# One step list reordered: the second sample pass's states, keys and values move from unit 5's u rows to its v rows, and its output norms go ahead of the attention

## The chip, the cores and the metric

The kernel runs on one core of one Trainium2 chip. The metric is device time in microseconds (us) of one execution. The kernel before was timed three times: 4341.75, 4350.58 and 4363.11 us, median 4350.58.

## The reference, cut to what matters

Two groups of tokens, a prompt of 128 and a sample of 512, run through two layers with shared weights. For the kernel these are four passes: p = 0 prompt layer 0, p = 1 sample layer 0, p = 2 prompt layer 1, p = 3 sample layer 1. A layer computes

```
h   = rmsnorm(x) * (1 + scale1) + shift1 ; proj = h @ w_in
o_f, o_b = chunk_gla(q, logf, v, S0)           # gated recurrence, forward and backward, 8 heads of 64x64 state
o   = rmsnorm(o_f + o_b) * silu(gate)          # the "output norm"
ckv = rmsnorm(ckv_raw); k_nope, v_att = ckv @ w_kvb    # keys and values from the latents
attn = softmax(q_nope k_nope + q_pe k_pe) v_att
x   = x + gate1 * (concat(o, attn) @ w_out)
h2  = rmsnorm(x) * (1 + scale2) + shift2
x   = x + gate2 * peer(h2)                     # 8 heads x 16 experts per token: rows of u and of v
```

The expert layer takes, for each token, 128 rows of the table u (a dot product each) and 128 rows of v (a weighted sum). All is float32.

## The kernel before, in words

Tokens are worked in tiles of 128, called units. Pass 0 is unit 0, pass 1 units 1 to 4, pass 2 unit 5, pass 3 units 6 to 9. Unit 5 is thus the prompt tile of layer 1; beside its expert rows the sample's layer 1 (pass 3) is prepared, as pass 1 is beside the rows of unit 0.

The expert rows are the backbone of the time. For each unit 128 gathers of u rows and then 128 of v rows are issued by GpSimd, each an indirect DMA of 128 rows of 4 KB into one of ten slots (`ring`, L853). VectorE reads a landed u slot in one multiply-reduce (`dots`, L1818) and so frees it; TensorE reads landed v slots in chunks of two (`sum_v`, L1170, eight recorded matmuls a chunk) and so frees them. This gives two stages for a unit: the u stage, paced by VectorE or the gathers, and the v stage, paced by TensorE or the gathers.

All other work, called trunk here, is woven between these rows by hand. `plan()` builds one list of steps (`PLAN`). Every engine walks that same list in order and does its part of each step, so the list fixes the order within each engine, while semaphores order the engines against each other. `beside_u[u]` and `beside_v[u]` name the trunk steps of the stages of unit u, each with a weight. `spread(a, b)` puts both lists on a line from 0 to 1 by their weights, each step at its middle, and merges them: 64 row steps of two rows each beside a trunk of total weight W lie W/64 apart. `spread_pairs(a, b)` merges two trunk lists and gives every step the weight 3.

The steps that the change touches:

- `keys_values(p)`: `wb` and `stores` (SyncE only; `wb` loads the attention's weights and waits for the last scan alone), `hgS` (VectorE carries the states over the tiles, L1628 and L1629), four `hgo` (TensorE applies the states, L1017, VectorE adds the result to `o`, L1641), `latT` (TensorE turns the normed latents, L901, ScalarE copies), `kn` (keys, L1041) and `va` (values, L1050), both TensorE with ScalarE copies. Weights 5 + 4 x 2 + 12 + 12 + 9 = 46.
- `outputs(p)`: four `hgfin`, the output norm of a tile: seven VectorE operations (L1653 to L1660) and a root on ScalarE. Weight 4 each.
- `keys_values_outputs(p)`: the same steps, two norms between `kn` and `va` and two after. It is used already for pass 1, beside the rows of unit 0.
- `attention(p, t)`: `q` (queries), then for eight heads `sc` (scores), `pt` (turned probabilities) and `pv` (sum over values). Weight 48.
- `("keys", p)`: SyncE loads the expert sub-keys over the attention's weights (L817), after a wait for the last `va` step; the next tiles of w_out stand behind it in SyncE's queue.
- `decided(p)`: `joined` (gate row L913, output projection, norm), eight steps of the expert query projection, two score steps, and eight top-k steps on VectorE, four of them between the two scores. Weight 138.

Of the kernel before, what the change touches and what calls it, by code (L numbers as in the profile page):

```python
# [32 lines left out]
N_IN, N_OUT, N_WQ = 26, 8, 16  # L33
# [36 lines left out]
def modulations(l, lo, hi):  # L70

    out = []
    for j in range(lo, hi):
        out.append((("ada", l, j), 1.5))
        if j % (3 * SECT) == 2 * SECT - 1:
            out.append((("adafin", l, j // (3 * SECT)), 1))
    return out


def norms(p, b):  # L80

    out = []
    for t in range(*BATCHES[p][b]):
        out += [(("rms", p, t, 0), 4), (("norm", p, t, 0), 4)]
    return out


def projections(p, b, lo=0, hi=N_IN):

    t0, t1 = BATCHES[p][b]  # L90
    out = [(("inp", p, b, j), 2 * max(1, (t1 - t0) * 0.9)) for j in range(lo, hi)]
    if hi == N_IN:
        out.append((("fgate", p, b), 4))
        out += [(("small", p), 0)] if b == 0 else []
        out += [(("rows", p), 0), (("latn", p), 3 + 3 * NT[p])] if b == len(BATCHES[p]) - 1 else []
    return out
# [12 lines left out]
def scans(p, t0, t1):  # L109

    return [(("hg", p, t, m), 4) for t in range(t0, t1) for m in range(LV)]


def keys_values(p):

    nt, g = NT[p], PASSES[p][0]
    out = [(("wb", p), 0), (("stores", p), 0)] if p else []
    if g:
        out += [(("hgS", p), 5)] + [(("hgo", p, t), 2) for t in range(nt)]
    return out + [(("latT", p), 3 * nt), (("kn", p), 12 if g else 4), (("va", p), 9 if g else 2)]  # L120


def keys_values_outputs(p):

    steps, gated = keys_values(p), outputs(p)
    half = (len(gated) + 1) // 2
    return steps[:-1] + gated[:half] + steps[-1:] + gated[half:]


def outputs(p):  # L130

    return [(("hgfin", p, t), 4) for t in range(NT[p])]


def attention(p, t):

    out = [(("q", p, t), 8), (("sc", p, t, 0), 2), (("sc", p, t, 1), 2), (("pt", p, t, 0), 2)]
    for hh in range(H):
        if hh + 2 < H:
            out.append((("sc", p, t, hh + 2), 2))  # L140
        out.append((("pv", p, t, hh), 1))
        if hh + 1 < H:
            out.append((("pt", p, t, hh + 1), 2))
    return out
# [7 lines left out]
def joined(p, t):  # L152

    tiles = served(p, t)
    return [(("outp", p, t, i), 5 * len(tiles)) for i in range(N_OUT // WCH)] \
        + [step for a in tiles for step in ((("rms", p, a, 1), 4), (("norm", p, a, 1), 6))]


def searched(p, t):

    return [(("wq", p, t, i), 5 * len(served(p, t))) for i in range(N_WQ // WCH)] \
        + [(("score", p, t, i), 3) for i in range(2)]


def queries(p, t):

    return joined(p, t) + searched(p, t)


def choice(p, t):  # L170

    u = U0[p] + t
    return [(("topk", u, hh), 7.5) for hh in range(H)] + [(("soft", u), 2)]


def opened(p):

    steps, heads = searched(p, 0), choice(p, 0)
    half = N_WQ // WCH // 2
    first, second, scores = steps[:half], steps[half:2 * half], steps[2 * half:]  # L180
    return joined(p, 0) + first + scores[:1] + heads[:1] + second[:2] + heads[1:2] + second[2:] + scores[1:]


def decided(p):

    steps, heads = searched(p, 0), choice(p, 0)
    half = N_WQ // WCH // 2
    first, second, scores = steps[:half], steps[half:2 * half], steps[2 * half:]
    return joined(p, 0) + first + scores[:1] + woven(heads[:4], second) + scores[1:] + heads[4:]


def spread(a, b, until=1.0):

    def placed(steps):
        total, at, out = sum(us for _, us in steps), 0.0, []
        for step, us in steps:
            out.append(((at + us / 2) / total, step))
            at += us
        return out

    merged = sorted([(x, 0, i, step) for i, (x, step) in enumerate(placed(a))]
                  + [(x * until, 1, i, step) for i, (x, step) in enumerate(placed(b))])
    return [step for _, _, _, step in merged]


def spread_pairs(a, b):

    return [(step, 3) for step in spread(a, b)]


def woven(a, b):

    us = dict(a + b)
    return [(step, us[step]) for step in spread(a, b)]


def first_unit():

    heads, rows = choice(0, 0), [(("u", 0, c), 2.6) for c in range(NCU)]
    ahead, beside = 2 * (H - 2), NCU * 17 // 20  # L220
    opening = []
    for hh in range(2, H):
        opening += rows[2 * (hh - 2):2 * (hh - 1)] + heads[hh:hh + 1]
    levels = scans(1, 0, NT[1])
    ends, last = LV - 1, (NT[1] - 1) * LV
    trunk = woven(levels[:ends], late_projections(1, LATE, 16)) \
        + woven(levels[ends:last + 3], late_projections(1, 16, N_IN)) + late_latents(1) + levels[last + 3:]
    return [("hp", 0)] + spread(opening + heads[H:], projections(1, 0, 0, LATE)) + [("fgate", 1, 0)] \
        + spread(rows[ahead:beside], trunk) + spread(rows[beside:], keys_values_outputs(1))


def plan():

    def alone(steps):
        return [step for step, _ in steps]

    first = modulations(0, 0, 2 * SECT)
    rms, norm = norms(0, 0)
    inputs = projections(0, 0)
    out = alone(first[:4] + [(("x0",), 0)] + first[4:12] + [rms] + first[12:] + [norm] + inputs[:6]  # L240
                + [(("rest",), 0)] + inputs[6:12] + [(("wb", 0), 0)])
    out += spread(inputs[12:N_IN], norms(1, 0)) + alone(inputs[N_IN:])
    out += spread(scans(0, 0, 1), modulations(0, 2 * SECT, 3 * SECT))
    out += spread(keys_values(0) + [(("keys", 0), 0)] + spread_pairs(attention(0, 0), outputs(0)),
                  modulations(0, 3 * SECT, N_ADA))
    out += alone([(("stores", 0), 0)] + opened(0))
    prompt_q = queries(2, 0)
    beside_u = {1: attention(1, 1) + queries(1, 1)[:-2],
                2: spread_pairs(attention(1, 3), modulations(1, N_ADA // 2, N_ADA)) + queries(1, 2),
                3: keys_values(2) + spread_pairs(attention(2, 0), outputs(2)) + [(("keys", 1), 0), (("score", 1, 3, 0), 3), (("score", 1, 3, 1), 3)],  # L250
                4: norms(3, 0) + projections(3, 0),
                5: norms(3, 1) + projections(3, 1, 0, 12) + [(("fgate", 3, 1), 4)]
                + woven(scans(3, 3, 4), projections(3, 1, 12, N_IN)[:N_IN - 12]) + [(("rows", 3), 0), (("latn", 3), 15)]
                + keys_values(3),
                6: attention(3, 1) + queries(3, 1)[:-2], 7: attention(3, 3) + joined(3, 2)}
    beside_v = {0: attention(1, 0) + [(("keys", 1), 0)] + decided(1),
                1: queries(1, 1)[-2:] + spread_pairs(choice(1, 1), spread_pairs(modulations(1, 0, N_ADA // 2), attention(1, 2))),
                2: spread_pairs(choice(1, 2), norms(2, 0) + projections(2, 0, 0, 20)) + projections(2, 0, 20)
                + scans(2, 0, 1),
                3: [(("keys", 2), 0)] + spread_pairs(choice(1, 3), prompt_q[:-2]) + prompt_q[-2:] + choice(2, 0),  # L260
                4: scans(3, 0, 3),
                5: spread_pairs(attention(3, 0), outputs(3)) + [(("keys", 3), 0)] + decided(3),
                6: queries(3, 1)[-2:] + spread_pairs(choice(3, 1), attention(3, 2)), 7: searched(3, 2) + choice(3, 2),
                8: [(("score", 3, 3, 0), 3), (("score", 3, 3, 1), 3)] + choice(3, 3),
                9: [(("y", u), 3) for u in range(NU - 5, NU - 1)]}
    for u in range(NU):
        rest = [(("u", u, c), 1) for c in range(NCU)]
        if u == 0:
            out += first_unit()
        else:  # L270
            out += [("hp", u)] + spread(rest, beside_u.get(u, []))
        out.append(("gelu", u))
        out += spread([(("v", u, c), 1) for c in range(NCV)], beside_v[u])
        out.append(("fin", u))
    return out + [("y", NU - 1)]


PLAN = plan()


# [1676 lines left out]
```

How the kernel before makes its waits and increments, by code:

```python
        @block.sync  # L754
        def _(sp):
            for dst, src in consts:
                sp.dma_start(dst, src).then_inc(s_const, 16)
            n = 0
            for k, step in enumerate(PLAN):
                name, a = step[0], step[1:]
                while n < len(WEIGHTS) and WEIGHTS[n][3] == k:
                    array, index, _, _ = WEIGHTS[n]
                    if W_OLD[n] is not None:
                        which, value = WEIGHTS[W_OLD[n]][2]
                        sp.wait_ge(C[which], value)
                    src = A[array]
                    for i in index:
                        src = src[i]
# [2 lines left out]
                    n += 1  # L771
                if name == "x0":
                    sp.dma_start(x[:, 0, :], A["x"][:, 0, :]).then_inc(s_x0, 16)
                elif name == "rest":
                    for dst, src in rest:
                        sp.dma_start(dst, src).then_inc(s_rest, 16)
                elif name == "small":
                    p, = a
                    g, l = PASSES[p]
                    if g:
                        sp.wait_ge(C["it"], after(("score", p - 1, NT[p - 1] - 1, 1), "it"))
                        sp.wait_ge(C["tk"], U0[p])
                        sp.wait_ge(C["tp"], after(("soft", U0[p] - 1), "tp"))
                        sp.dma_start(ckv[:, 0, :], A["cache_ckv"][l]).then_inc(s_sw, 16)
# [42 lines left out]
            sp.wait_ge(s_Sst, 16 * 2)  # L827
            sp.wait_ge(s_yst[0], 16 * 3)
            sp.wait_ge(s_yst[1], 16 * 2)
```

## Time and profile before

| what | value |
|---|---|
| median of three runs | 4350.58 us |
| the profiled execution's own time | 4343.34 us |
| its span, first to last instruction | 4341.5 us |
| TensorE (matmul) busy | 2725.6 us, 63% |
| VectorE busy | 2653.9 us, 61% |
| GpSimd busy | 2439.9 us, 56% |
| ScalarE busy | 690.8 us, 16% |
| DMA, HBM read | 1579.27 MB, 365 GB/s over the span |
| mean granted TensorE clock | 0.759 of full speed |

Busy shares are means over stages with different limits. The stages of one unit follow each other, so a change to one stage is read from the table of that stage: how long it lasts, which engine has no gaps in it, and what the others wait for.

### The profile page before, as it was taken

Reading aid. Unit: us, or ns where it says so; the run is one execution under the profiler, and the core shown is the slowest. Engines: PE = TensorE matmul, PEld = TensorE weight load, DVE = VectorE, ACT = ScalarE, POOL = GpSimd, SP = SyncE. Lnnn points to the kernel's source line nnn. Section 1 sums busy time; section 2 is a strip of 40 time slices with the busy share of each in tenths; the row PEclk is TensorE's granted clock in tenths of the full one; section 3 lists DMA queues with packets and bytes.
Section 4 is the critical chain, followed back from the end, with each engine's and each line's share of the span. In section 5 each row is a group of like instructions: output and inputs, shape, how many; then the busy total and the mean of one; then the engine's idle time right before and its main releaser. Section 6 shows DMA issues by size and latency. Waiting matters only on the chain. (4 is left out here: it accounts for less than half of the span.)

```text
span 4341.5 us, 54057 instructions
## 1 busy us (share of the span) xinstructions
PE 2725.6 (63%) x20238; PEld 1717.4 (40%) x20238; DVE 2653.9 (61%) x6612; ACT 690.8 (16%) x1551; POOL 2439.9 (56%) x2565
## 2 busy tenths in 40 slices
PE   8888858764668776147695565866576476045046
PEld 7656734353336743133382263445423452000000
DVE  2268861586448653976775388259747916991940
ACT  3313322011111112110102222201011100000000
POOL 0023425565655465656656655656576656777775
PEclk9699869767976888568797876976786687566566
DMA  8566758999999999999999999999999999999998
GB/s 306 171 226 224 256 190 317 381 385 419 405 384 415 365 400 364 407 395 415 369 417 385 366 406 359 374 362 345 417 394 392 397 378 389 416 419 408 417 420 361
DMA packets 456819, 1586.36 MB, mean 365 GB/s; under 512 B 71152, under 2 KB 73456, under 8 KB 455280
## 3 DMA queue, kind: packets, MB, share of 16 engines
q0 software_dynamic: 368640, 1342.34, 78.4%
q1 hardware_dynamic: 87920, 240.56, 14.6%
q8 instruction: 163, 2.67, 0.2%
q14 instruction: 96, 0.79, 0.0%
HBM read 1579.27 MB, written 3.44 MB: 365 GB/s over the span
## 5 line engine op out<-in xcount | busy, mean ns | idle before, releaser
L853 POOL DMA_INDIRECT ring<-in_peer_u,eidx x1280 | 1213.9, 948 | 1158.3 <-DVE dot L1818 656.9
L853 POOL DMA_INDIRECT ring<-in_peer_v,eidxT x1280 | 1225.6, 958 | 720.3 <-PE acc L1170 380.5
L1818 DVE CUSTOM_DVE_ANT_0 ring<-ring,acc 128x1024 f32<-128x1024 f32 x1280 | 1508.9, 1218 | 158.6 <-DMA ring<-in_peer_u,eidx 132.0
L1170 PE MATMUL acc<-ring,wz 128*32 128x512 f32 x5120 | 848.1, 752 | 440.2 <-DMA ring<-in_peer_v,eidxT 430.2
L1170 PEld LDWEIGHTS acc<-ring,wz 128*32 128x32 f32 x5120 | 132.3, 119 | 921.3 <-issue 869.7
L1124 PE MATMUL pp<-hT,wring 128*128 128x128 f32 x2304 | 302.8, 295 | 48.4 <-DMA wring<-in_w_q 47.1
L1124 PEld LDWEIGHTS pp<-hT,wring 128*128 128x128 f32 x2304 | 290.3, 208 | 89.0 <-DMA wring<-in_w_q 53.0
L901 PE MATMUL tb<-ident,gl 128*128 128x128 f32 x10 | 4.5, 446 | 442.0 <-DVE gl L1825 442.0
L1763 DVE MAX8 v<-lat 128x8 f32<-128x128 f32 x160 | 38.8, 284 | 292.1 <-ACT lat L1210 282.2
L936 PE MATMUL pp<-hT,wring 128*128 128x128 f32 (+2 forms) x768 | 204.9, 432 | 13.1 <-DMA wring<-in_w_in 8.8
L901 PEld LDWEIGHTS tb<-ident,gl 128*128 128x128 f32 x10 | 1.7, 174 | 445.5 <-DVE gl L1825 445.5
L942 PE MATMUL pp<-wring,hT 128*128 128x128 f32 (+1 forms) x1120 | 154.0, 303 | 32.6 <-DMA wring<-in_w_in_tail 13.4
L936 PEld LDWEIGHTS pp<-hT,wring 128*128 128x128 f32 x768 | 128.3, 210 | 99.0 <-issue 59.9
L942 PEld LDWEIGHTS pp<-wring,hT 128*128 128x128 f32 x1120 | 148.0, 217 | 46.9 <-issue 26.5
L901 PE MATMUL tb<-ident,xn 128*128 128x128 f32 (+1 forms) x240 | 48.5, 369 | 176.9 <-DVE xn L1539 135.8
L1120 PE MATMUL pp<-wring,hT 128*128 128x128 f32 x1152 | 139.9, 281 | 28.2 <-DMA wring<-in_w_out 20.8
L1120 PEld LDWEIGHTS pp<-wring,hT 128*128 128x128 f32 x1152 | 133.3, 194 | 41.0 <-DMA wring<-in_w_out 25.2
L1726 DVE TENSOR_REDUCE mx<-pp 128x1 f32<-128x640 f32 (+1 forms) x80 | 57.3, 716 | 134.0 <-PE pp L1073 134.0
L954 PE MATMUL pp<-wring,hT 128*128 128x128 f32 (+1 forms) x896 | 120.0, 292 | 15.7 <-DVE h L1602 10.9
L1073 PE MATMUL pp<-U,hT 96*128 96x128 f32 (+1 forms) x272 | 127.7, 610 | 2.9 <-ACT hT L1210 2.8
L954 PEld LDWEIGHTS pp<-wring,hT 128*128 128x128 f32 x896 | 111.7, 204 | 20.7 <-DVE h L1602 12.0
L1210 ACT ACTIVATE hT<-tb 128x512 f32<-128x512 f32 (+4 forms) x152 | 67.3, 471 | 313.4 <-PE tb L901 298.3
(276 smaller groups left out, 3617.0 us busy)
## 6 DMA issues: line engine op xcount, KB each, us to landing
wring<-in_w_q SPq DMA_DIRECT2D x123, 512.0 KB
wring<-in_w_in SPq DMA_DIRECT2D x110, 512.0 KB
wring<-in_w_ada SPq DMA_DIRECT2D x66, 512.0 KB
wring<-in_w_out SPq DMA_DIRECT2D x59, 512.0 KB
ring<-in_peer_u,eidx POOLq DMA_INDIRECT x1280
ring<-in_peer_v,eidxT POOLq DMA_INDIRECT x1280
ring<-in_w_ada SPq DMA_DIRECT2D x30, 512.0 KB, 6.6
ring<-in_w_in SPq DMA_DIRECT2D x15, 512.0 KB, 8.0
```

What stands on the lines that cost most here:

```text
L853: pool.indirect_dma_start(ring[:, G_SLOT[n], :], None, A[table], bass.IndirectOffsetOnAxis(ap=rows, axis=0),).then_inc(s_g[G_SLOT[n]], 16)
L901: ins = nc.tensor.transpose(tb[0:m, b, i * P:(i + 1) * P], piece, ident[:, :])
L936: ins = nc.tensor.matmul(out[:, 0:n], wt[:, c, :], h[:, c, 0:n], start=(c == 0), stop=(c == KC - 1))
L942: ins = nc.tensor.matmul(out[:, (t - t0) * P:(t - t0) * P + m], h[:, c, (t - t0) * P:(t - t0 + 1) * P], wt[:, c, 0:m], start=(c == 0), sto ...
L954: ins = nc.tensor.matmul(out[:, 0:m], hT[:, c, t * P:(t + 1) * P], open_tile[:, c, 0:m], start=(c == 0), stop=(c == KC - 1))
L1073: ins = nc.tensor.matmul(b[:, k0:k0 + kn], turned_queries(p)[0:DQ, hh, :], kT[0:DQ, hh, k0:k0 + kn], start=True, stop=True)
L1120: project_chunk(p, t, i, "id", lambda out, w, m, c: nc.tensor.matmul(out, m, w, start=(c == 0), stop=(c == KC - 1)))
L1124: project_chunk(p, t, i, "ia", lambda out, w, m, c: nc.tensor.matmul(out, w, m, start=(c == 0), stop=(c == KC - 1)))
L1170: ins = nc.tensor.matmul(acc[32 * q:32 * q + 32, half * 512:(half + 1) * 512], wz[:, at:at + 32], row[:, half * 512:(half + 1) * 512], sta ...
L1210: return nc.scalar.activation(dst, src, ACT.Copy, **kw)
L1726: link(v.tensor_reduce(mx[:, hh % 2, :], pp[:, n % 2, 0:keys], AX.X, ALU.max))
L1818: v.tensor_tensor_reduce(rows, rows, acc[:, :], 1.0, 0.0, ALU.mult, ALU.add, dot[:, n:n + 1])\
```

## The change

In the u stage of unit 5, `keys_values(3)` is dropped from the trunk. In its v stage, the interleaving of the first attention tile with the output norms is replaced by `keys_values_outputs(3)` followed by the attention alone, at its own weights. No instruction is added or removed; order and spacing change.

```diff
                 5: norms(3, 1) + projections(3, 1, 0, 12) + [(("fgate", 3, 1), 4)]
-                + woven(scans(3, 3, 4), projections(3, 1, 12, N_IN)[:N_IN - 12]) + [(("rows", 3), 0), (("latn", 3), 15)]
-                + keys_values(3),
+                + woven(scans(3, 3, 4), projections(3, 1, 12, N_IN)[:N_IN - 12]) + [(("rows", 3), 0), (("latn", 3), 15)],
                 6: attention(3, 1) + queries(3, 1)[:-2], 7: attention(3, 3) + joined(3, 2)}
...
                 4: scans(3, 0, 3),
-                5: spread_pairs(attention(3, 0), outputs(3)) + [(("keys", 3), 0)] + decided(3),
+                5: keys_values_outputs(3) + attention(3, 0) + [(("keys", 3), 0)] + decided(3),
```

## Rows read from the trace of the kernel before

**Rows 1.** Waits of GpSimd, whole kernel: us in total, times, longest us

```profile
POOL ring L853 <- DVE dot L1818: 705.3, 608, 21.9
POOL ring L853 <- PE acc L1170: 393.5, 310, 16.9
```

**Rows 2.** Busy time by stretch: the u stage of the last unit, without trunk work

```profile
core 0: us, PE busy (x) PEld busy (x) DVE busy (x) ACT busy (x) POOL busy (x), PEclk, DMA share, GB/s
4007.00:4163.00 156.00, 0.00 (x0) 0.00 (x0) 152.71 (x255) 1.40 (x2) 116.42 (x125) 0.50 1.01 410
```

**Rows 3.** Busy time by stretch: unit 5's stages, and the front of unit 0's v stage

```profile
2488.90:2650.00 161.10, 84.05 (x768) 78.65 (x768) 144.13 (x285) 31.80 (x76) 91.74 (x94) 0.70 0.99 385
2650.00:2698.20 48.20, 39.73 (x207) 26.89 (x207) 43.12 (x74) 18.81 (x28) 28.51 (x31) 0.72 0.88 326
2698.20:2771.60 73.40, 62.33 (x373) 27.98 (x373) 28.02 (x75) 25.75 (x52) 49.24 (x51) 0.91 1.00 397
2771.60:2930.10 158.50, 114.86 (x792) 71.92 (x789) 68.48 (x285) 13.46 (x26) 77.57 (x82) 0.82 0.93 361
643.40:706.10 62.70, 50.85 (x309) 25.67 (x309) 16.56 (x52) 18.93 (x43) 31.04 (x34) 0.90 0.81 307
```

**Rows 4.** VectorE's groups, end of unit 5's u stage (2646.9 to 2698.2)

```profile
L1818 DVE CUSTOM_DVE_ANT_0 ring<-ring,acc 128x1024 f32<-128x1024 f32 x35 | 40.3, 1216 | 0.1
...
L1641 DVE TENSOR_TENSOR o<-pp,o 128x512 f32<-128x512 f32 x4 | 2.8, 692 | 4.9 <-PE pp L1017 4.9
L1629 DVE TENSOR_TENSOR hT<-xn,hT 128x512 f32<-128x512 f32 x3 | 2.1, 692 | 0.1
L1628 DVE TENSOR_TENSOR xn<-hT,Dt 128x512 f32<-128x512 f32 x2 | 1.4, 692 | 0.1
L1628 DVE TENSOR_TENSOR xn<-S,Dt 128x512 f32<-128x512 f32 x1 | 0.7, 686 | 0.0
```

**Rows 5.** Line L1818, 2488.9 to 2650: its operations, and what VectorE waited for

```profile
L1818 DVE CUSTOM_DVE_ANT_0 ring<-ring,acc x94: 1214/1218/1223, 2488.9 to 2645.8; 128x1024 f32<-128x1024 f32 x94
...
  DMA ring<-in_peer_u,eidx: 8.2, 8
```

**Rows 6.** Busy time by stretch: hgo; latT; kn; va in unit 5's u stage

```profile
2651.30:2665.30 14.00, 13.89 (x129) 13.80 (x129) 9.18 (x15) 0.00 (x0) 5.62 (x6) 0.50 0.83 277
2665.30:2676.40 11.10, 6.51 (x29) 3.95 (x28) 10.91 (x18) 8.95 (x14) 6.55 (x7) 0.65 0.64 218
2676.40:2686.90 10.50, 10.50 (x32) 5.57 (x33) 10.50 (x21) 4.19 (x6) 7.78 (x9) 0.83 1.01 394
2686.90:2695.90 9.00, 8.83 (x22) 3.57 (x21) 9.00 (x17) 3.92 (x7) 6.86 (x8) 1.00 1.03 419
```

**Rows 7.** TensorE in order of time, unit 5: two v chunks; gate row; soft step

```profile
2714.15 1.94 PE L1170 MATMUL acc<-ring,wz 128*32 128x512 f32 x8
...
2718.06 1.07 PE L1170 MATMUL acc<-ring,wz 128*32 128x512 f32 x8
...
2771.61 2.05 PE L913 MATMUL pp<-ident,mods 128*128 128x128 f32 x16
...
2925.50 0.47 PE L901 MATMUL tb<-ident,lat 128*128 128x128 f32 x1 [11.08 <-DVE lat L1801]
```

**Rows 8.** TensorE's v-row matmuls by group, 643.4 to 706.1 (unit 0)

```profile
L1170 PE MATMUL acc<-ring,wz 128*32 128x512 f32 x136 | 19.6, 656 | 1.3 <-ACT hT L1210 0.7 <-ACT wz L1210 0.6
```

**Rows 9.** TensorE in order of time, unit 0's v stage: queries and gate row

```profile
650.79 4.99 PE L1058 MATMUL pp<-wqb,hT 128*128 128x384 f32 x12
...
706.13 2.05 PE L913 MATMUL pp<-ident,mods 128*128 128x128 f32 x16
```

**Rows 10.** Waits of TensorE, 2771.6 to 2889.5 (unit 5, gate row to second score)

```profile
PE acc L1170 <- DMA ring<-in_peer_v,eidxT: 8.2, 3, 4.1
```

**Rows 11.** VectorE in order of time: first top-k after the second score

```profile
2892.79 0.49 DVE L1763 MAX8 v<-lat 128x8 f32<-128x128 f32 x2 [13.44 <-ACT lat L1210]
```

**Rows 12.** SyncE's queue in order of time: sub-keys, w_out behind them

```profile
2695.76 0.34 SPq L817 DMA_DIRECT2D wkvb<-in_keys  x1
2696.15 92.52 SPq L770 DMA_DIRECT2D wring<-in_w_out  x8
```

## The prediction, made before the changed kernel was run

> **What bounds the kernel now.** I read the waits of GpSimd first, since it issues the gathers that go on through nearly the whole run. It waits 705.3 us for slots that VectorE has yet to free and 393.5 us for slots of TensorE [rows 1]. So neither the transfers nor one engine bounds the run: in a u stage VectorE mostly does, in a v stage TensorE, and both share a floor. The floor stands in the u stage without trunk work: 125 gathers in 156.0 us at a DMA share of 1.01, or 1.25 us a gather [rows 2], 160 us for 128.
>
> Next, the busy table of unit 5's stages [rows 3]. The reader is to see four stretches. From 2488.9 to 2650 the u rows run beside projections and a scan: 94 rows in 161.1 us with the DMA share at 0.99. The weight tiles take what the gathers leave, so this stretch is full for the DMA engines. From 2650 to 2698.2 the block that moves runs: the DMA share falls to 0.88 while VectorE is busy 43.12 us of 48.20. From 2698.2 to 2771.6 the attention runs beside v rows: TensorE busy 62.33 of 73.40 us, VectorE 28.02. From there to 2930.1, the finish, stands the chain of output projection, expert queries and top-k.
>
> I work in three terms: what the u stage gets back, what the front of the v stage (dots' end to the gate row) gains in length, and what its rest gives back.
>
> **Term 1, the u stage.** Leaving it: three carry steps of two operations of 0.69 us (groups of 3, 2 and 1), four additions to o of 0.69 us, and 4.9 us for which VectorE stands in front of these additions waiting for TensorE [rows 4]. That is 4.2 + 2.8 + 4.9, some 12 us with the small gaps. The check: the last 128 - 94 = 34 dots at 1.142 us start to start (40.3 us for 35 busy, the pipelined readout inside) need 38.8 us, and they ended 51.2 us after the block began at 2647; the rest is 12.4. Keys, values and turned latents cost this stage nothing: VectorE has no part in them and runs dot after dot beside them. If VectorE stays the bound, the stage gives 12.4 us.
> It may not. The same 34 rows are now spread beside projections and scan, where transfers are full [rows 3]; there each costs the gather's 1.25 us, 42.5 us together, and 51.2 - 42.5 leaves a gain of only 9. VectorE already waits 8.2 us there for gathers [rows 5]. I take 10, between 4 (that wait grows by more) and 12.4.
> SyncE is hardly touched: the load of attention weights waits only for the last scan, not for its place in the list. The sub-key load and the w_out tiles behind it [rows 12] wait for the last value step; they will start some 60 us into the v stage and are needed at its 120th, so I cost that at nothing. Were it late, TensorE would wait at the gate row.
>
> **Term 2, the front of the v stage.** Step positions follow from the weights. Before: total 225, a chunk each 3.52, and 87 weight before the gate row: 25 chunks. After: total 62 + 48 + 138 = 248, a chunk each 3.875. By the middles of the steps, 17 chunks fall before the attention's queries, 12 between these and the gate row, 29 in all.
>
> - The block itself, on TensorE: 14.0 us for hgo, 11.1 for latT, 10.5 for kn, 9.0 for va, 44.6 us [rows 6]. I keep those durations, slow clock included: hgo ran at a granted clock of 0.50 after TensorE had stood idle, and it will have stood idle again, since the list leaves it nothing between the last scan and the end of the dots.
> - Ahead of it: two chunks while VectorE does the carries, until 5.8 us after the dots.
> - The other 15 chunks before the queries: three at the slow 1.94 us and twelve at 1.07 [rows 7], 18.7 us. No gather is late here: 34 in 69 us, against 42 at the floor.
> - The output norms: VectorE and ScalarE alone, four of 5 us in the 20 us of kn and va plus their chunks, with VectorE otherwise free. Hidden. Without that cover each would put 5 us ahead of the queries.
> - The attention with 12 chunks. The nearest row is unit 0's v stage, which has this very attention without norms between: from the queries at 650.8 to the gate row at 706.1 [rows 9], 55.3 us with 16 of its 17 chunks (136 matmuls of 8 [rows 8]). Four chunks fewer at 1.07 give 51.0.
>
> Sum: 5.8 + 44.6 + 18.7 + 51.0 = 120.1 us, against 73.4 now: **+46.7**. From below: hgo at full clock saves 7 and the three slow chunks 2.6. From above: with fewer chunks the attention waits for its own chain, score to maximum to exponential, and keeps its 55.3: +4.3.
>
> **Term 3, the rest of the v stage.** Between gate row and second score 29 chunks stood; by the new spacing 26 do. Three at 1.07 us are 3.2 us. TensorE also waits 8.2 us for v gathers there [rows 10]. A TensorE-bound front leaves all ten slots full at the gate row, which at the floor is 12 us of transfer in hand, so most of that wait should go. VectorE can follow an earlier second score: it idled 13.44 us before it [rows 11]. After it four top-k heads on VectorE end the stage, and TensorE already idles 11.08 us for them [rows 7]; nothing changes there. I take -8, between -3 and -13.
>
> **Sum.** -10 + 46.7 - 8 = +28.7 us. The profiled execution took 4343.3 us (span 4341.5 and 1.8 around it): 4372 after. The median of the runs shown is 7.3 us above that execution, so on that scale I forecast 4350.6 + 28.7 = **4379**.
>
> **Rivals.**
> - *The block is absorbed (faster).* TensorE is without matmuls for 11 us of the front and, with the rest, for 55 us of the v stage's 231.9 [rows 3]. If the moved matmuls pipeline with the v rows and only fill gaps, the gathers keep pacing the front: 29 chunks of two at 1.25 us are 72.5 us, no more than now. Then term 1 (-10) and term 3 (-8 to -13) remain, -21 in the middle: 4330. For it: matmul spans overlap, and weight loads are busy only 27.98 of 73.40 us. Against it: unit 0's front, with eight chunks fewer, is 10.7 us shorter (62.7 against 73.4 [rows 3]), so each chunk taken away shortened it, by more than its own 1.07 us; a full engine does that, a half-empty one does not. It decides from the point where the front stays under 91 us, 73.4 and the 18 of the other terms. The Trainium skill, "Perfetto Trace Analysis", section "Identifying the Most-Contended Engine", says that matmul busy time misjudges TensorE's room and that the busy share of weight loads is to be read instead; by that rule the front has 62% of TensorE free and this rival would be the forecast, 4330. The unit 0 row disagrees. Chance 0.13.
> - *Half absorbed (within 0.5%).* Clock high from the start (-9.6), five ScalarE waits of latT hidden, term 3 at -13, term 1 at -12: +12, or 4362. Speaks for it that the v stage feeds TensorE right from its start. Chance 0.22.
> - *Starved (slower still).* Term 1 gives 4, the attention does not shrink, term 3 gives 3: 46.7 + 4.3 - 4 - 3 = +44, 4395. Chance 0.12.
> - The forecast: 0.53.
>
> That the steps do not move as said can be left out: every engine walks the one list.
>
> **Range and chances.** The forecast's own range is 4366 to 4390. With the others, 4348 to 4397 holds 8 in 10. A measurement of this kernel tells about 0.5%, 22 us, from no change, so slower means above 4372. The forecast lies above that in most of its range (0.49 of its 0.53), the starved case wholly; the half absorbed case is within, the absorbed one, at -21, is split between faster and within. A little of every case is left for what I do not see, in both directions. Rounded: faster 0.11, same 0.28, slower 0.61.
>
> **What would show it.** After the change the last 34 dots run without carries between them, and the u stage is 197 to 205 us instead of 209.3. hgo starts some 6 us after the dots at a granted clock near 0.5. The gate row stands 115 to 125 us after the dots instead of 73.4. In the front, GpSimd waits for TensorE much longer and the DMA share falls well under the present 1.00. Between gate row and second score the waits for v gathers nearly vanish. Term 1 is wrong if VectorE's waits for u gathers grow by over 8 us; term 2 is wrong if the front stays under 105; the whole is wrong if unit 5's u and v stage together are not longer. Another unit's stages should not change.

## The result, and the profile after

The changed kernel takes 4364.4 us (median of 20 runs, 4337.05 to 4379.01) against 4346.2 us of the kernel before (20 runs, 4326.6 to 4363.1). The ratio is 1.0038, 95% interval [1.0024, 1.0051]: slower by 16.5 us, with the sign as forecast and 57% of the size (+28.7). 4364.4 is inside the range that was to hold 8 in 10 (4348 to 4397) and 1.6 us below the forecast's own (4366 to 4390); on the scale of the prediction, 4350.6 times the ratio, it is 4367. It stays within the 0.5% that was called no change, so the likeliest of the three outcomes (slower by more, 0.61) did not come.

The profiled execution took 4352.6 us, 9.2 more than that of before. Only unit 5 is rearranged, so its stages are read first. Busy time by stretch, changed kernel: dots until the last scan's end, the 39 us without TensorE work, the front of the v stage, and its rest. Columns as in [rows 3].

```profile
2490.10:2651.20 161.10, 83.61 (x768) 78.08 (x768) 145.50 (x255) 31.45 (x75) 102.68 (x105) 0.73 0.99 398
2651.20:2690.30 39.10, 0.00 (x0) 0.00 (x0) 36.22 (x94) 1.49 (x2) 19.90 (x22) 0.50 1.02 385
2690.30:2799.65 109.35, 94.84 (x612) 48.30 (x612) 34.85 (x85) 36.97 (x75) 56.08 (x58) 0.91 0.86 310
2799.65:2942.80 143.15, 104.46 (x759) 66.53 (x756) 68.23 (x285) 14.61 (x26) 68.41 (x72) 0.86 0.91 356
```

Beside [rows 3]: the u stage ends 200.3 us after its first dot instead of 209.3. TensorE now sits idle for the last 39 of these, at a granted clock of 0.50. The front takes 109.3 us instead of 73.4, and the DMA share there fell from 1.00 to 0.86: the gathers no longer pace it. The rest takes 143.2 instead of 158.5. Sum: -9.0 + 35.9 - 15.3 = +11.6 us. The rest of the run, all other units together, changed by -2.4 us, no unit's by more than about 4.

The waits of GpSimd over the whole run show the same exchange (us in total, times, longest), beside [rows 1]:

```profile
POOL ring L852 <- DVE dot L1817: 683.5, 604, 21.9
POOL ring L852 <- PE acc L1169: 442.1, 345, 17.1
```

22 us less on VectorE, 49 us more on TensorE. And line L1817 in unit 5's u stage, beside [rows 5], with what VectorE waited for:

```profile
L1817 DVE CUSTOM_DVE_ANT_0 ring<-ring,acc x128: 1211/1216/1222, 2490.1 to 2689.1; 128x1024 f32<-128x1024 f32 x128
...
  DMA ring<-in_peer_u,eidx: 14.5, 16
```

The waits for gathers went from 8.2 to 14.5 us: part of what VectorE was relieved of went to the transfers.

TensorE in order of time, front of the changed v stage:

```profile
2692.27 3.64 PE L1169 MATMUL acc<-ring,wz 128*32 128x512 f32 x16 [0.68 <-ACT wz L1209]
2695.84 0.70 PE L1016 MATMUL pp<-S,U 64*128 64x64 f32 x4
...
2697.97 2.23 PE L1016 MATMUL pp<-hT,U 64*128 64x64 f32 x36
...
2721.47 8.92 PE L1040 MATMUL pp<-hT,wkvb 128*128 128x512 f32 x32
...
2734.75 9.00 PE L1049 MATMUL pp<-wkvb,hT 128*128 128x512 f32 x20
...
2748.53 4.14 PE L1057 MATMUL pp<-wqb,hT 128*128 128x384 f32 x12
```

The reader is to see that hgo (L1016) starts slow, four matmuls in 0.70 us, and is fast two microseconds later, 36 in 2.23 us; at a granted clock of 0.50, in e9 below, 32 take 3.73 us. In the u stage of before it stayed at 0.50 for its whole 14 us [rows 6]. The queries start 58.2 us after the dots, not 69.1, and from there to the gate row it takes 51.1 us; the forecast was 51.0.

### The profile page after: what moved, and what is told of

Read it like the earlier page. It is cut to its first block and busy times, and to the rows that moved or that the text cites. A ratio compares the mean times of both kernels' runs of the same rounds, so it can differ in the third digit from the quotient of the medians.

```text
span 4350.8 us, 54052 instructions
## 1 busy us (share of the span) xinstructions
PE 2712.3 (62%) x20238; PEld 1711.5 (39%) x20238; DVE 2654.6 (61%) x6612; ACT 685.2 (16%) x1547; POOL 2436.2 (56%) x2565
## 3 DMA queue, kind: packets, MB, share of 16 engines
q1 hardware_dynamic: 87920, 240.56, 14.5%
## 5 line engine op out<-in xcount | busy, mean ns | idle before, releaser
L1817 DVE CUSTOM_DVE_ANT_0 ring<-ring,acc 128x1024 f32<-128x1024 f32 x1280 | 1510.6, 1218 | 167.2 <-DMA ring<-in_peer_u,eidx 137.0
L935 PE MATMUL pp<-hT,wring 128*128 128x128 f32 (+2 forms) x768 | 205.1, 432 | 14.5 <-DMA wring<-in_w_in 10.2
L953 PE MATMUL pp<-wring,hT 128*128 128x128 f32 (+1 forms) x896 | 119.9, 292 | 15.6 <-DVE h L1601 10.8
L953 PEld LDWEIGHTS pp<-wring,hT 128*128 128x128 f32 x896 | 111.6, 204 | 20.6 <-DVE h L1601 12.0
L900 PEld LDWEIGHTS tb<-ident,xn 128*128 128x128 f32 (+1 forms) x240 | 39.9, 191 | 191.2 <-DVE xn L1538 141.0
```

What stands on the lines that cost most here:

```text
L900: ins = nc.tensor.transpose(tb[0:m, b, i * P:(i + 1) * P], piece, ident[:, :])
L935: ins = nc.tensor.matmul(out[:, 0:n], wt[:, c, :], h[:, c, 0:n], start=(c == 0), stop=(c == KC - 1))
L953: ins = nc.tensor.matmul(out[:, 0:m], hT[:, c, t * P:(t + 1) * P], open_tile[:, c, 0:m], start=(c == 0), stop=(c == KC - 1))
L1817: v.tensor_tensor_reduce(rows, rows, acc[:, :], 1.0, 0.0, ALU.mult, ALU.add, dot[:, n:n + 1])\
```

## The experiments

Each kernel was timed in five rounds beside the kernel before; ratios are to that, with 95% intervals. One profile of each gave the stage lengths. "Front" is the end of the dots to the gate row, "middle" gate row to second score. The table holds all of them (us, chunks of v rows in brackets). The kernel before has one profile too, and its unit 5 may be a long one: in all 13 others the change of its two stages together lies below what the ratio says, by 0.6 to 12 us, 6.7 on average.

| kernel | ratio | u stage | front | middle | v stage |
|---|---|---|---|---|---|
| before | 1 | 209.3 | 73.4 (25) | 118.0 (29) | 231.9 |
| change | 1.0038 [1.0024, 1.0051] | 200.3 | 109.3 (29) | 102.6 (26) | 252.5 |
| e1_kv_only | 1.0084 [1.0056, 1.0112] | 200.2 | 127.6 (32) | 100.0 (24) | 268.0 |
| e2_norms_only | 1.0031 [1.0015, 1.0046] | 207.9 | 72.8 (21) | 121.8 (32) | 235.1 |
| e3_left_out_before | 0.9974 [0.9956, 0.9992] | 200.1 | 73.1 (25) | 113.2 (29) | 226.8 |
| e4_left_out_after | 0.9996 [0.9979, 1.0014] | 200.4 | 72.5 (21) | 121.7 (32) | 234.8 |
| e5_change_again | 1.0040 [1.0021, 1.0059] | 199.9 | 107.6 (29) | 103.5 (26) | 251.7 |
| e6_more_rows_in_tail | 0.9979 [0.9963, 0.9995] | 208.4 | 68.3 (24) | 114.2 (26) | 223.1 |
| e7_same_middle | 1.0077 [1.0057, 1.0097] | 200.6 | 114.8 (25) | 111.6 (29) | 266.9 |
| e8_only_keys_and_values | 1.0038 [1.0017, 1.0059] | 207.4 | 93.7 (25) | 114.8 (29) | 249.1 |
| e9_one_chunk_ahead | 1.0083 [1.0065, 1.0100] | 200.4 | 119.9 (29) | 106.0 (26) | 266.4 |
| e10_two_chunks_ahead | 1.0054 [1.0034, 1.0074] | 200.2 | 102.4 (25) | 110.7 (29) | 253.6 |
| e11_tail_and_spaced_hgo | 0.9967 [0.9951, 0.9983] | 203.0 | 69.1 (24) | 110.7 (26) | 219.7 |
| e12_change_and_tail | 1.0049 [1.0030, 1.0068] | 201.1 | 107.0 (27) | 101.9 (25) | 249.4 |

**The two halves of the change.** e1 moves the block and leaves attention and norms woven:

```diff
-                5: keys_values_outputs(3) + attention(3, 0) + [(("keys", 3), 0)] + decided(3),
+                5: keys_values(3) + spread_pairs(attention(3, 0), outputs(3)) + [(("keys", 3), 0)] + decided(3),
```

> keys_values(3) moves to the v rows of unit 5 as in the change, but the attention and the output norms stay interleaved at weight 3 as before. Theory (the moved block itself is the price, on TensorE): about the change's result, +10 to +20 us over before; front of the v stage (dots' end to gate row) 105 to 118 us, u stage about 200. Rival (the norms ahead and the attention at its own weights are the price): within 5 us of before, since that part is undone, and the front under 95 us.

It came out at +36 us, nearly twice my upper end and worse than the change itself, with a front of 127.6 us where I had 118 at most. The rival is refuted, but my theory did not say why undoing half of the change makes it slower. That is taken up below.

e2, against the kernel before, moves only the norms:

```diff
-                5: spread_pairs(attention(3, 0), outputs(3)) + [(("keys", 3), 0)] + decided(3),
+                5: outputs(3) + attention(3, 0) + [(("keys", 3), 0)] + decided(3),
```

> keys_values(3) stays beside the u rows; only the output norms go ahead of the attention, at their own weights. Theory: u stage 209 as before; the front about 73 (norms now uncovered, some 18 us on VectorE, but 5 chunks fewer), the rest of the stage longer by 5 to 10 us, since 33 chunks instead of 29 fall between gate row and second score: +3 to +10 in all. Rival: most of the change's +16 us is here, +14 to +20.

The front came as expected, 72.8 us. The rest of the stage grew by 3.8 us where I had 5 to 10, though its middle is 8.6 us longer than e3's (113.2). The total, +13 us, lies above the expected end, and its interval (+7 to +20) reaches into both the theory's range and the rival's. In the one profile unit 5 is only 1.8 us longer than before, so most of the +13 is not placed.

**The block's price on either side.** e3 and e4 leave the work of keys_values(3) out, in the order of before and in that of the change. Its weight loads stay, with a wait for them ahead of the sub-key load and of the first queries:

```diff
 e3: in the u stage
-                + keys_values(3),
+                + [(("wb", 3), 0)],
 e4: in the v stage
-                5: keys_values_outputs(3) + attention(3, 0) + [(("keys", 3), 0)] + decided(3),
+                5: [(("wb", 3), 0)] + outputs(3) + attention(3, 0) + [(("keys", 3), 0)] + decided(3),
```

> Leaves out the work of keys_values(3) (states carried, added, latents turned, keys, values of the last pass), so that its attention reads stale data; the weight loads stay. Otherwise the order of before. Prices the block in the u stage. Theory: u stage 197 to 201 us (9 to 12 us less, as in the change), v stage as before at 232 us, total -9 to -12. Rival (the u stage is bound by transfers beside the projections, the block was nearly free there): total within 4 us of before, VectorE's waits for u gathers grow by as much as the block gave.

> Leaves out the same work from the order of the change: norms ahead, then the attention, nothing of keys_values(3) but its weight loads; rows are spaced by a total weight of 202. Prices the block in the v stage. Theory: u stage about 200, v stage about 235 to 242 (as the kernel with only the norms ahead), so total -2 to +2 against before and 12 to 20 us under the change. Rival (the block was mostly absorbed among v rows): within 6 us of the change.

e3's u stage is 200.1 us, the same as in every kernel that has no part of the block there (199.9 to 201.1). So the block costs that stage 9.2 us, and 11.3 in the whole run. Its rival was half true in its mechanism: the waits for u gathers grew to 15.0 us. e4 has the same u stage; from e4 to the change the ratio rises by 0.0042, 18 us. So the block costs 11 us beside u rows and 18 us beside v rows. The remaining difference, e3 to e4, is 0.0022 or 9.6 us: norms ahead of the attention, with no block to cover them and the rows spaced anew. In the stages it is 8.0 us, all of it in the middle, which got three more chunks. The three are steps of one path from before to the change, so that they sum to the result (-11.3 + 9.6 + 18.3 = +16.6 us) tells nothing new. Each is uncertain by 8 to 11 us as a ratio, and 9.6 is not clear of nothing; that the block is dearer beside v rows rests on the stages, where it takes 9.2 us of the u stage and adds 16.9 to 17.7 to the v stage (234.8 in e4, 251.7 and 252.5 with the block).

**Was the fast clock luck?** The front was 11 us shorter than forecast, and nearly all of that lies in the block. e5 is the changed kernel again. e7 scales its front so that 25, 29 and 10 chunks fall as before:

```diff
-                5: keys_values_outputs(3) + attention(3, 0) + [(("keys", 3), 0)] + decided(3),
+                5: [(s, us * 87 / 110) for s, us in keys_values_outputs(3) + attention(3, 0)] + [(("keys", 3), 0)] + decided(3),
```

> The changed kernel a second time, on the chip of the three kernels beside it. It asks how steady the parts are that one profile showed: u stage of unit 5 200.3 us, front of its v stage 109.3, gate row to second score 102.6, and the states applied (hgo) in 8 us at full clock. If the front's shortness against the forecast of 120 was luck of the clock, hgo takes 14 us at half clock this time and the front is near 118; if it belongs to the order, 109 and 8 come again. Time: 1.003 to 1.005 of before.

> The change's order, with the weights of its front scaled by 87/110, so that 25 chunks fall in the front, 29 between gate row and second score and 10 behind it, as before the change. Theory (spacing): the middle stretch takes 110 to 114 us instead of 102.6, the front 105 (four chunks fewer at 1.07), stage +4 against the change. Rival (the full ring at the gate row gave the middle its time): middle stays under 105. One chunk instead of two stands before the first hgo here; if the rows ahead of it raise the clock, hgo runs at half clock and the front is 6 us longer than that.

e5 repeats the change in all parts, its hgo again at full clock. In e7 the middle grows to 111.6 us, 8 to 9 more for three chunks, as the theory of spacing has it. But its front is longer than the change's, 114.8 against 109.3, with four chunks fewer. In e7, and in e1, rounding of the spacing puts only one chunk ahead of the first hgo. e9 and e10 test that alone, by swapping two neighbours in the finished list:

```diff
 e9, from the change: hgo ahead of the second chunk
+    i = out.index(("hgo", 3, 0))
+    out[i - 1:i + 1] = [out[i], out[i - 1]]
 e10, from e7: the second chunk ahead of hgo
+    i = out.index(("hgo", 3, 0))
+    out[i:i + 2] = [out[i + 1], out[i]]
```

> The change with two neighbouring steps of unit 5's v stage swapped: the first hgo stands ahead of the second v chunk, so one chunk (not two) precedes the state matmuls. Nothing else moves. Theory (two chunks in a row raise TensorE's clock, the small state matmuls alone do not keep or raise it): hgo from first to last start takes 17 to 18 us (8.5 in the change), front of the v stage 116 to 119 us instead of 108 to 109, total +8 to +10 us over the change, 1.006 of before. Rival (the clock at that place is chance, or set by the total spacing): hgo 8 to 9 us, front and time as the change.

> The kernel with the change's front scaled to 25 chunks, with the second chunk swapped ahead of the first hgo. Theory: the reverse of the swap above, hgo 8 to 9 us (17.8 without the swap), front about 105 us instead of 114.8, total about 9 us less than without it, 1.0055 to 1.006 of before. Rival (chance or total spacing): hgo near 18 us again, 1.0077 of before.

TensorE in order of time at that place, e9:

```profile
2700.95 1.94 PE L1172 MATMUL acc<-ring,wz 128*32 128x512 f32 x8 [0.68 <-ACT wz L1212]
2704.12 0.70 PE L1019 MATMUL pp<-S,U 64*128 64x64 f32 x4 [1.24 <-DVE hT L1631]
...
2709.62 3.73 PE L1019 MATMUL pp<-hT,U 64*128 64x64 f32 x32
...
2721.60 0.69 PE L1019 MATMUL pp<-S,U 64*128 64x64 f32 x4
2722.22 3.64 PE L1172 MATMUL acc<-ring,wz 128*32 128x512 f32 x16
```

And e10:

```profile
2698.78 3.18 PE L1172 MATMUL acc<-ring,wz 128*32 128x512 f32 x16 [0.68 <-ACT wz L1212]
2701.95 0.45 PE L1019 MATMUL pp<-S,U 64*128 64x64 f32 x4
...
2703.53 4.01 PE L1019 MATMUL pp<-hT,U 64*128 64x64 f32 x68
```

Busy time by stretch over hgo, e9 and then e5:

```profile
2704.10:2722.20 18.10, 18.08 (x144) 14.45 (x144) 2.08 (x3) 0.00 (x0) 4.69 (x5) 0.50 0.61 212
```

```profile
2706.20:2714.70 8.50, 8.50 (x140) 7.54 (x136) 2.08 (x3) 0.00 (x0) 4.67 (x5) 1.00 0.91 326
```

The theory held in both directions. With one chunk ahead, TensorE is busy 18.08 of 18.10 us with small state matmuls and single chunks and stays at 0.50; with two it reaches 1.00. The swap alone costs the front 11 to 12 us and the run 0.0045 (about 19 us, twice the expected 8 to 10). The reverse swap gives back 12.4 us of front and 0.0023 (10 us) of the run; the two intervals overlap, so there the front is the evidence. e1 belongs to the same group. Its block took 61.4 us with 11 chunks, the change's 58.2 with 17. Against e9, which also has one chunk ahead, e1 shows no difference (1.0084 and 1.0083, each within 0.003), so with the block there, weaving norms and attention changes nothing that these runs can tell.

**Keys and values alone.** e8 leaves states, hgo and latT beside the u rows:

```diff
+                + keys_values(3)[:-2],
...
+                5: keys_values_outputs(3)[8:] + attention(3, 0) + [(("keys", 3), 0)] + decided(3),
```

> States, their application and the turned latents stay beside the u rows; only keys and values move to the v rows, the norms again ahead of the attention. Theory (VectorE's part alone is what the u stage gets back; keys and values cost it nothing): u stage 208 to 210 us as before, front about 85 us, v stage 238 to 244, unit 5 in all +6 to +12 over before with no gain to set against it. Rival (TensorE's whole block slows the u stage through shared transfers and semaphores): u stage 203 or less.

The u stage got back 1.9 us at most and the v stage paid 17. So keys and values cost next to nothing beside the dots. The total, 1.0038 or +16.5 us, is above the +6 to +12 that I expected. The front was 93.7 us, 9 over the expectation. TensorE in order of time ahead of its queries:

```profile
2747.17 1.94 PE L1170 MATMUL acc<-ring,wz 128*32 128x512 f32 x8 [5.55 <-DMA ring<-in_peer_v,eidxT]
2749.04 6.27 PE L1058 MATMUL pp<-wqb,hT 128*128 128x384 f32 x12
```

A v gather came 5.55 us late, and the queries behind it ran slow, 6.27 us for the same 12 matmuls that took 4.14 in the change. I had expected no late gather there; what delayed it was not followed further.

**A version that beats both.** Behind the second score, VectorE's four top-k heads take 40.6 us whatever TensorE does (40.4 to 40.7 in all but e11). TensorE idled 11 us of that [rows 7]. e6, from the kernel before, gives these heads more weight, so that 14 chunks, not 10, fall there. e11 adds u rows between the hgo steps; e12 applies the first to the change, two chunks kept ahead of hgo:

```diff
 e6 and e11 (e12 likewise, after the change's own front)
-                5: spread_pairs(attention(3, 0), outputs(3)) + [(("keys", 3), 0)] + decided(3),
+                5: spread_pairs(attention(3, 0), outputs(3)) + [(("keys", 3), 0)] + decided(3)[:-5] + [(s, 12) for s, _ in decided(3)[-5:-1]] + decided(3)[-1:],
 e11 only
-                + keys_values(3),
+                + [(s, 4 if s[0] == "hgo" else us) for s, us in keys_values(3)],
```

> Everything as before the change, but the last four top-k heads of unit 5's v stage weigh 12 instead of 7.5, so that 14 chunks of v rows (not 10) fall behind the second score and 26 (not 29) between gate row and second score, 24 (not 25) in the front. Theory (between gate row and second score transfers bind, each chunk there costs about 2.7 us, while behind the second score VectorE's top-k binds and 14 chunks still fit): v stage 222 to 226 us instead of 232, total -6 to -10. Rival (what the change gave back there was the full ring or the clock, not the spacing): within 3 us of before.

> The kernel with more v rows behind the second score (0.998 of before), and in unit 5's u stage the four hgo steps weigh 4 instead of 2, so that u rows stand between all of them. Theory (VectorE stood 4.9 us in front of the four additions while TensorE was still at the state matmuls): with rows between, these waits fall under 1.5 us, the u stage takes 204 to 206 us instead of 208 to 209, total 0.997 of before. Rival (that time is given back to the gathers): u stage unchanged, waits for u gathers up by as much.

> The change with the last four top-k heads at weight 12 (27 chunks in the front, 25 between gate row and second score, 12 behind), and the first hgo still behind two chunks. Theory (a chunk costs 1.1 us in this front, 2.8 between gate row and second score, nothing behind): v stage 247 to 249 us instead of 252, total 3 to 5 us less than the change, 1.003 of before and clearly above the kernel that keeps the block beside the u rows. Rival (the spacing does nothing once the ring is full): as the change, 1.004.

The last stretch of the v stage, second score to finish, in e6:

```profile
2890.25:2930.92 40.67, 26.94 (x147) 9.26 (x148) 32.57 (x143) 3.45 (x6) 28.36 (x30) 0.72 1.02 417
```

30 gathers at a DMA share of 1.02 in a stretch no longer than before. e6 gained 9 us, as expected in size, but not where the theory put it: the front gave 5.1 and the middle 3.8, and its middle with 26 chunks (114.2; e11: 110.7) is hardly shorter than the middles with 29 in e3 and e8 (113.2, 114.8). What TensorE waited for in that middle:

```profile
PE acc L1170 <- DMA ring<-in_peer_v,eidxT: 10.3, 4, 3.9
PE pp L1124 <- DMA wring<-in_w_q: 5.5, 2, 2.9
```

Its front is paced by gathers, so it enters the middle with an emptier ring: counted from the DMA packets, 1.5 of the ten slots hold a landed row at the gate row and 6.4 at the second score, where the change has 6.4 and 2.6. About 57 gathers thus land in e6's middle and 48 in the change's, though TensorE reads 52 rows in both. The change, e5 and e9, with the same 26 chunks and 6.3 or 6.4 landed rows at the start, took 102.6, 103.5 and 106.0 us. The state at the entry alone does not tell the length: e8 entered with 6.5 and took 114.8, with 56 gathers landing. e11 has the lowest ratio, 0.9967 [0.9951, 0.9983], 14 us under the kernel before; its interval overlaps e6's. VectorE's waits in its u stage have none left for the additions to o (4.9 us in e6):

```profile
DVE U L1551 <- ACT U L1253: 8.1, 1, 8.1
DVE ring L1818 <- DMA ring<-in_peer_u,eidx: 5.7, 8, 1.3
DVE ring L1818 <- DVE x L1840: 0.8, 1, 0.8
```

Its u stage, 203.0 us, is 5.4 under e6's. On e12 the expectation failed in time: its v stage is 2 to 3 us shorter than the change's in the profile, but the ratio, 1.0049, is not below 1.0038. The intervals overlap; whether it gains at all stays open.

## Why the prediction was right in sign and over in size

**Term 1, -10: right.** -9.0 in the profile, -9.4 in the repeat, and 9.2 by leaving the work out (e3). Both bounds acted together, as argued: 12.4 us of VectorE left, and its waits for gathers took 6.3 of that back. That alone would make 6.1. Two waits for ScalarE of before, 4.5 and 1.4 us (L1551, L1565), are gone too, which I had not counted, and small gaps between operations and less overlap take about 3 back. So the size owes something to luck.

**Term 2, +46.7: the mechanism right, the block mis-sized.** The front grew by 35.9 us (34.2 in e5). The part behind the queries was exact, 51.1 for 51.0 (50.3 in e5). The part before them took 58.2 us for 69.1, and so the gate row stood 109.3 us after the dots, outside the 115 to 125 that I gave as a sign. The step that failed is "I keep those durations, slow clock included". hgo took 8.1 us without its inner chunk where I had 14.0, latT and kn 2.7 less together, and the chunks among them ran at full clock sooner. I had the reason for the slow start right (TensorE idle 39 us, clock 0.50 at the first matmul) but not what ends it. My lower bound held this case as 7 + 2.6 us. e9 shows the price of the case that I forecast: with one chunk ahead the queries start 68.8 us after the dots, against my 69.1, and hgo without its two inner chunks takes 14.4 us.

**Term 3, -8: right in sign, under in size.** -15.3 in the profile. Part of that is the reference: the middle of before was a long one, 118.0 us at a clock of 0.86, where e3, with the same order there, took 113.2. From 113 the change gives about -10, and the three terms, -9 + 36 - 10, make about the +16.5 that the timed runs show; the one profile of before would account for the 5 us between +11.6 and +16.5. That is an inference from e3 and from the 13 profiles that all lie on that side of their ratios, not from a repeat of the kernel before, and the order by bytes below speaks against it: there the middle of before is on the line and e3's is the one that is off. How much of -15.3 is the reference stays open. What I had wrong in the working is the price of a chunk. I took TensorE's 1.07 us and set the transfer apart as "8.2 us of waits that should go". The 14 middles order badly by chunks: 26 chunks took 102.6, 103.5, 106.0, 110.7 and 114.2 us, 29 took 110.7 to 118.0. They order well by what was moved. In 13 of them the transfers ran at 353 to 371 GB/s (389 in e3), at a DMA share of 0.92 to 0.97; rate times length is 36.7 MB in the change, 38.3 in e9, 40.4 in e7, 41.2 in e6, 42.8 in the kernel before and 45.2 in e2 (121.8 us). So the middle follows its bytes, 2.7 to 2.8 us for each MB, and a chunk, two gathers of 0.52 MB, costs about 3 us there rather than 1.07. It also gains or pays what the ring drains or fills in it: the ring held 6.4 landed rows at the gate row, not the ten of my argument, and 2.6 at the second score. And the waits did not vanish, they fell from 8.2 to 6.6 us.

**The rivals.** Absorption (4330) fell: the front, 109.3 us, went far over its limit of 91. By the rule of the Trainium skill ("Perfetto Trace Analysis", "Identifying the Most-Contended Engine"), weight loads busy 38% of the old front meant room. The traces disagree. From e4 to the change the block and eight chunks more went into a front of 72.5 us with weight loads busy 37%; the front grew by 36.8 us, and the matmuls' busy time by 35.7 (59.2 to 94.8), while weight loads were still busy only 44%. The front followed the matmul spans, not the loads. "Half absorbed" (+12) named the clock rightly and is nearer to +16.5 than my forecast. Its waits of latT for ScalarE were not hidden, though: between 2706.7 and 2716.8 us TensorE was busy 4.75 of 10.10 us. The +12 does not contain them either; -12 + 46.7 - 9.6 - 13 makes 12 without that part.

**The sub-key load.** It moved to 53 us into the v stage, and TensorE waited for w_out's tiles 1.9 us in the middle, 2.3 before. Costed at nothing, rightly.

## What to carry to other kernels

Price a moved step by the engine that is full where it lands, and take the price of its neighbours too: here the same block costs 9 to 11 us beside VectorE-bound rows and 17 to 18 beside TensorE-bound ones. Where an engine restarts after idling, look at the first operations of the new order; one swap of neighbours was worth as much as the whole change. Where a fixed chain ends a stage (here top-k), fill the time beside it before rearranging anything else.

## What the runs showed of the hardware that I had not expected

TensorE, busy 18.08 of 18.10 us, stayed at half its clock when its work was 64x64 state matmuls with single v chunks between (e9), and was at full by hgo's start or within 2 us of it when two v chunks in a row stood ahead (the change, e5, e10, e12). A trace without gaps on TensorE thus did not mean the full clock here. hgo from its first to its last state matmul took 8.3 to 8.8 us in the profiles with two chunks ahead and 17.8 us in all three with one (e1, e7, e9). In the three with one chunk, TensorE also stood idle for 1.2 us between that chunk and hgo, waiting for VectorE's carried states; with two there was no such gap. The runs do not separate the second chunk from the gap, so why two suffice and one does not stays open.
